# Loading the gate table and gating the first two head pairs inside the last ticks of the stick-breaking attention

## The reference, cut to what matters

```python
q, g = jnp.split(h @ w_in_b[j], 2, axis=-1)
o = _stick_breaking_attention(q, k, v)        # 8 heads of 64, 4 query blocks of 128
o = o.transpose(0, 2, 1, 3).reshape(bsz, seq, ATT_WIDTH)
x = x + (o * jax.nn.silu(g)) @ w_out_b[j]
return _rmsnorm(x, norm_f)

# inside the attention, for one query block:
z = jnp.einsum("bhqd,bhkd->bhqk", qb, kf[:, :, :kl]) * scale
log_one_minus = jnp.where(mask, jax.nn.log_sigmoid(-z), 0.0)
rev = lax.cumsum(log_one_minus, axis=3, reverse=True)
weights = jnp.exp(jnp.where(mask, z + rev, -jnp.inf))
outs.append(jnp.einsum("bhqk,bhkd->bhqd", weights, vf[:, :, :kl]))
```

## Time and profile before

| what | value |
|---|---|
| median of three runs | 1260.31 us (1258.64 to 1261.17) |
| the profiled execution | 1260.45 us, of which 1258.7 us are the span of its instructions |
| TensorE matmul busy | 1165.2 us, 93% of the span |
| VectorE busy | 752.7 us, 60% |
| ScalarE busy | 617.9 us, 49% |
| GpSimd busy | 484.8 us, 39% |
| mean granted TensorE clock | 0.973 |

### The profile page before, as it was taken

How to read it: one execution, slowest core, us unless ns; L and a number is a source line. 1 busy time by engine, 2 the same in 40 slices (tenths; PEclk the granted TensorE clock), 3 DMA queues, 4 the chain that set the end, 5 groups by cost and what they waited for, 6 DMA issues and landing times.

```text
span 1258.7 us, 19508 instructions
## 1 busy us (share of the span) xinstructions
PE 1165.2 (93%) x7570; PEld 901.6 (72%) x7570; DVE 752.7 (60%) x1179; ACT 617.9 (49%) x1018; POOL 484.8 (39%) x391
## 2 busy tenths in 40 slices
PE   5899899997886899899999998999999999999977
PEld 4665667676773687677777776777888888867656
DVE  4775996793556536566766656364285234567753
ACT  4667453633553336656656464364221244466655
POOL 1432334355760244323333334443444445532321
PEclk8999899998998899999999999999999999999988
DMA  6742245427005162221221222522333333222111
GB/s 235 251 113 67 68 102 149 131 88 194 12 4 172 34 191 85 84 67 56 77 67 55 67 84 68 165 86 69 99 100 90 96 100 101 84 76 60 52 33 67
DMA packets 198909, 119.49 MB, mean 95 GB/s; under 512 B 27741, under 2 KB 187174, under 8 KB 198566
## 3 DMA queue, kind: packets, MB, share of 16 engines
q1 hardware_dynamic: 197312, 116.08, 31.4%
q10 hardware_dynamic: 1510, 2.20, 0.5%
HBM read 103.06 MB, written 15.20 MB: 94 GB/s over the span
## 4 chain that ended last, share of the span: by engine, by line
PE 38%; issue 29%; POOL 15%; DVE 12%; ACT 2%; DMA 2%; SPq 0%; POOLq 0%; ACTq 0%; DVEq 0%
POOL b_w_lo L547 13%; PE banks L625 10%; PE banks L626 10%; PE banks L627 10%; DVE b_problems L2077 2%; DVE b_sum_squares L2075 1%; PE banks L1193 1%; DVE b_a_lo L1937 1%; PE banks L632 1%; PE banks L1221 1%; POOL b_sum_squares L592 1%; DVE b_sum_squares L2010 1%; DMA b_spread_heads<-spread_heads 1%; DVE b_suffix L2523 1%; POOL b_squares L584 1%
## 5 line engine op out<-in xcount | busy, mean ns | idle before, releaser
L547 POOL TENSOR_TENSOR b_w_lo<-b_w_raw,b_w_hi 128x512 fp32r<-128x512 f32 x320 | 428.9, 1361 | 717.3 <-ACT b_w_hi L1291 717.2
L625 PE MATMUL banks<-b_a_lo,b_w_hi 128*128 128x512 f32 x1280 | 525.0, 410 | 31.6 <-DVE b_a_lo L2190 12.7
L627 PE MATMUL banks<-b_a_hi,b_w_lo 128*128 128x512 f32 x1280 | 505.5, 395 | 0.0
L626 PE MATMUL banks<-b_a_hi,b_w_hi 128*128 128x512 f32 x1280 | 504.7, 394 | 0.0
L625 PEld LDWEIGHTS banks<-b_a_lo,b_w_hi 128*128 128x128 f32 x1280 | 243.8, 190 | 110.5 <-issue 26.1
L1291 ACT ACTIVATE b_w_hi<-b_w_raw 128x1024 fp32r<-128x1024 f32 x160 | 168.7, 1055 | 252.4 <-PE banks L627 247.0
L627 PEld LDWEIGHTS banks<-b_a_hi,b_w_lo 128*128 128x128 f32 x1280 | 243.7, 190 | 53.9
L626 PEld LDWEIGHTS banks<-b_a_hi,b_w_hi 128*128 128x128 f32 x1280 | 244.6, 191 | 44.6
L1682 ACT ACTIVATE b_exps<-banks,b_stats 128x128 f32<-128x128 f32 (+3 forms) x64 | 33.2, 524 | 60.1 <-DVE b_stats L2313 60.1
L1617 ACT ACTIVATE b_a_hi<-b_x_t,b_params 128x512 fp32r<-128x512 f32 x48 | 33.9, 719 | 54.7 <-DVE b_x_t L2198 54.2
L2198 DVE TENSOR_TENSOR b_x_t<-b_x_t,banks 128x512 f32<-128x512 f32 x32 | 21.9, 686 | 60.7 <-PE banks L627 60.7
(11 more groups left out here) (315 smaller groups left out, 1512.4 us busy)
## 6 DMA issues: line engine op xcount, KB each, us to landing
b_w_raw<-rw_w_in SPq DMA_DIRECT2D x32, 512.0 KB, 4.4
b_w_raw<-da_w_in SPq DMA_DIRECT2D x32, 512.0 KB, 4.0
b_w_raw<-w_in_a SPq DMA_DIRECT2D x32, 512.0 KB, 4.0
b_w_raw<-pe_w_gate SPq DMA_DIRECT2D x16, 512.0 KB, 4.1
d_ple<-b_ple_out SPq DMA_DIRECT2D x16, 256.0 KB, 4.9
b_w_raw<-rw_w_out SPq DMA_DIRECT2D x8, 512.0 KB, 6.6
b_ple_in<-d_ple SPq DMA_DIRECT2D x2, 2048.0 KB, 10.3
b_w_raw<-da_w_out SPq DMA_DIRECT2D x8, 512.0 KB, 4.0
```

The source lines that it names most:

```text
L547: m = pool.tensor_tensor(WLO[:, u % 2, ks], WRAW[:, u, ks], WHI[:, u % 2, ks].bitcast(F32), ALU.subtract)
L625: pe.matmul(dst, hi, a_lo[:, k_act, :], start=first, stop=False)
L626: pe.matmul(dst, hi, a_hi[:, k_act, :], start=False, stop=False)
L627: return pe.matmul(dst, lo, a_hi[:, k_act, :], start=False, stop=last)
```

## The change: what it does

On ScalarE the load of the Silu table moves from behind the ticks into tick 21, directly behind the Exp of the last step's weights. The gates of pairs 0 and 1 follow it, ahead of the copy of the last transposed weights. The gate of pair 2 and the high parts of pairs 0 and 1 stand behind that copy, ahead of `hi` of the second slot of `w_out_b`. The gate of pair 3, two high parts and the square root's table come last, the table now behind the high parts. On VectorE the products of pairs 0 and 1 with their gates move ahead of the copy of the last transposed weights; the low parts of pairs 0 and 1 are made in a row behind the product of pair 2. TensorE, GpSimd and the DMA queues have the same instructions in the same order.

```diff
@@ ScalarE @@
+        def gate_of(j):
+            act.wait_ge(sem("bank_free"), n0 + 12 + j + 1)
+            act.activation(SGT[:, j, :], SGT[:, j, :], ACT.Silu).then_inc(sem("sg_done"), 1)
+
+        def split_pair(k):
+            act.wait_ge(sem("pair_gated"), k + 1)
+            split(1, k, SQT[:, k, :])
+
         for tick in range(1, SB_TICKS):
@@
             if 2 <= s < SB_STEPS + 2:
                 weights_of(s - 2)
+            if tick == SB_STEPS + 5:
+                act.preload_act_table_set("silu_and_others")
+                gate_of(0)
+                gate_of(1)
@@
             if 6 <= tick < SB_STEPS + 6:
                 keep_weights(tick - 6)
+            if tick == SB_STEPS + 5:
+                gate_of(2)
+                split_pair(0)
+                split_pair(1)
@@
             if q == 2 and 3 * p + 3 < len(SB_SLOTS) + 2:
                 hi(g0 + 3 * p + 3)
-        act.preload_act_table_set("silu_and_others")
-        for j in range(3):
-            act.wait_ge(sem("bank_free"), n0 + 12 + j + 1)
-            act.activation(SGT[:, j, :], SGT[:, j, :], ACT.Silu).then_inc(sem("sg_done"), 1)
-        for j in range(3, HT4):
-            act.wait_ge(sem("bank_free"), n0 + 12 + j + 1)
-            act.activation(SGT[:, j, :], SGT[:, j, :], ACT.Silu).then_inc(sem("sg_done"), 1)
+        gate_of(3)
+        split_pair(2)
+        split_pair(3)
         act.preload_act_table_set("sqrt_and_others")
-        for k in range(HT4):
-            act.wait_ge(sem("pair_gated"), k + 1)
-            split(1, k, SQT[:, k, :])
         hi(RUN_BO[0] + 2)
@@ VectorE @@
+        def gate_pair(k):
+            dve.wait_ge(sem("sg_done"), k + 1)
+            if k < HT4 - 1:
+                dve.wait_ge(sem("pair_out"), k + 1)
+                tt(SQT[:, k, :], SQT[:, k, :], SGT[:, k, :], ALU.mult).then_inc(sem("pair_gated"), 1)
+            else:
+                dve.wait_ge(sem("pair_mm"), SB_STEPS)
+                tt(SQT[:, k, :], BANK[7], SGT[:, k, :], ALU.mult).then_inc(sem("pair_gated"), 1)
+
+        def lo_pair(k):
+            split_lo(A_BO, 1, k, SQT[:, k, :])
+
@@
             if tick == SB_STEPS + 5:
+                gate_pair(0)
+                gate_pair(1)
                 keep_weights(SB_STEPS - 1)
-        for k in range(HT4):
-            ...
+        gate_pair(2)
+        lo_pair(0)
+        lo_pair(1)
+        gate_pair(3)
+        lo_pair(2)
+        lo_pair(3)
```

## The result

The changed kernel took 1253.60 us (median of 5 runs, 1249.86 to 1257.50) against 1260.31 (median of 5, 1256.09 to 1261.83). The ratio is 0.9946, with a 95% interval of 0.9924 to 0.9969: about 6.8 us faster, between 3.9 and 9.6. The profiled execution took 1253.60 us with a span of 1251.8; the one before had 1258.7.

A forecast was written before the change was run, and what follows sets the result against it. TensorE's 6.0 us wait before the first w_out_b product was the target. Gains of 2.3 (clock low, weighted twice) and 4.1 (up) gave 2.9; 1260.45 - 2.9 = 1257.5, median 0.14 lower: 1257.4 us, range 1254.5 to 1259.7.

The forecast's parts named there:

- What bounds the kernel, and the first product: TensorE's 6.0 us wait before the first w_out_b product; that product was to move 4.6 us earlier.
- both places without reserve: Load and two Silu before ScalarE's copy L1812, two products before VectorE's waiting copy: both were to fit at price 0.
- The turns between VectorE and GpSimd: Low parts 2 and 3 wait on GpSimd's instructions; of the 4.6 us, 0.5 is lost, leaving 4.1.
- The clock: TensorE's clock falling in the tail costs 1.8 us, leaving a 2.3 gain; held twice as likely as staying up.
- Ahead of the last Exp nothing moves: Everything before the tail, up to the last Exp, was to keep its times: no shift there.
- 0.3 for the spread of a median: Allowance for measurement spread, in the forecast's own lower end of 1255.9 us (clock up, 4.1).
- case A: VectorE and GpSimd do not meet; low parts 2 and 3 take 0.68 each: gain 5.8, 1254.5 us, chance 0.12.
- B: TensorE's clock falls late and stays low to 1228.3: gain 0.6, time 1259.7 us, chance 0.13.
- the low case: Clock low while the fourth group of matmuls and its followers run: 3.6 us at half speed cost 1.8, gain 2.3.
- C: Each ScalarE table switch waits about one load's length more, delaying copy L1812 by 1.25: gain 1.65, 1258.7 us, chance 0.05.
- D: ScalarE reloads a table around each Copy, five changes costing 6.4 us: time 1263.8 us, chance 0.04.
- E: The moves lose 0.3 to 0.5 us in each place without reserve: gain about 2, 1258.3 us, chance 0.06.

The follow-up runs named there:

- GpSimd's pair late: Changed kernel with the second w_out_b weight slot rounded behind the last high part, so GpSimd subtracts after the four low parts: 1254.87 us, ratio 0.9953.

## Why the prediction was wrong, point by point

**What bounds the kernel, and the first product.** Right. Counted from the last Exp's start, the first product was put at 5.85 and came at 5.84; both places without reserve (L1812 and VectorE's copy L2513) cost nothing.

**The turns between VectorE and GpSimd.** Right in kind, a little too dear. Low parts 2 and 3 were put at 1.27 and 1.94, and took 1.15 and 1.77. The fourth group was put at 10.13 and came at 9.75, 0.4 us earlier. The two runs that move GpSimd's pair show that its place decides which instructions of VectorE are slow.

**The clock: the mis-sized term of the tail.** "I hold that for twice as likely as the clock staying up", with 1.8 us for it. The price was right: 45.3 against 43.4 is 1.9. The odds were not borne out, as far as three profiles tell: two had the clock up. This took 1.2 us off the forecast that the first profile did not pay; with the 0.4 above, the fourth group was 4.5 us earlier instead of 4.1. Behind it the shift was pure to 0.1 us (4.4 at the end).

**The step that put the time out of the range** is "Ahead of the last Exp nothing moves", with "0.3 for the spread of a median" as its only allowance. True of what the change does, it is not true of two executions. The lower end of the range, 1254.5, is case A's 5.8 us taken off the old median, with nothing for executions of one program differing ahead of the change. Between two profiles of the kernel before the last Exp lies 5.0 us apart, and its runs spread over 11 us. Five runs of each left an interval of 3.9 to 9.6 us; the execution that is the changed kernel's median stood 2.5 us early at the last Exp.

**The miss, added up.** The forecast for the profile was 1257.5 and it took 1253.6: 2.5 ahead of the last Exp, 1.2 by the odds of the clock and 0.4 by cheaper turns, less the 0.1 lost behind the fourth group, make 4.0 against a miss of 3.9. With 12 runs and again 12, the medians were 1257.21 and 1257.64, against a forecast of 1257.4, and the gain over all runs 3.5 us against a forecast of 2.9. That does not make the range right, and that the later medians lie this near the forecast is in part luck: the chance before the tail is averaged out there, and the odds of the clock were a guess. It says that about 0.6 us of the miss can belong to the kernel, a difference that these runs can hardly tell from none, and that the rest is chance.

**Rivals.** A (no meeting) did not happen. B (low for longer) did happen in one profile of the changed kernel, in part: the clock came back at 13.7 behind the Exp, as early as in before, and cost no more than the low case. C (a switch dearer than its row) did not happen: the Silu row starts 0.01 us after the load's row ends. The Trainium skill ("ScalarE: Activation LUTs", What ACT_TABLE_LOAD costs) puts about 1380 ns of drain beside the load, and no such time shows here. D is refuted by the same rows: Copy runs between Silu with no further load. E cost nothing.

## What to carry to other kernels

Put a table load and the work behind it into a wait of the same engine, but lay out every engine's queue to the first consumer before trusting it: in the run with the loads alone the first high part came 2.8 us earlier, the first low part 2.0, the fourth group 1.8 and the end 0.9 to 1.4, as the next engine ran into a third one and the low clock took its share. Where operands arrive one by one and slowly, giving the matmul engine more work per operand (two output tiles at a time) brought another 2 to 3 us here. Making each operand faster (GpSimd's pair late) brought about as much, 2.4 by the medians, and both together no more. And let the range hold the spread of the measurement too, taken from many repeated executions of the kernel before, not from three.

## What the runs showed of the hardware that was not expected

The size of the spread in one unchanged program: 1253.96 to 1265.34 us in 35 runs, and 0.58 against 1.00 of granted clock over the same 12 us, a place that made 7.1 us between two executions. A filler that kept the clock up through a pause of 6 us gained 0.6 to 1.1 us in the profile and nothing that the timing could tell: where slow matmuls run ahead of late operands, as here, half speed was nearly free. Why the clock stayed up in two profiles of the changed kernel and fell in the third, with the same pauses to 0.02 us, was not settled.
